# The first MLP product of an encoder block as seven block products

## The reference, cut to what matters

```python
u = _rms(h, norm_mix[l])
proj = u @ w_in[l]                       # latents, convolution input, gates
...
h = h + (g_a * attn + g_c * conv) @ w_out[l]
u = _rms(h, norm_mlp[l])
h = h + jnp.square(jax.nn.relu(u @ w_mlp_in[l])) @ w_mlp_out[l]
return _rms(h, norm_final)[:, N_META:]
```

## Time and profile before

| | |
|---|---|
| median of 3 runs | 1289.13 us (1288.31 to 1291.43) |
| the profiled execution | 1290.69 us |
| its span, first to last instruction | 1289.1 us |
| mean granted TensorE clock | 0.994 |
| PE busy | 1251.3 us, 97% |
| DVE, ACT, POOL busy | 738.5, 490.5, 394.8 us |
| DMA | 146.55 MB, mean 114 GB/s |

### The profile page before, as it was taken

One profiled execution on the slowest core, in us unless ns is written; L12 is line 12 of the kernel. 1 busy time (PEld: TensorE's weight loads), 2 busy tenths in 40 slices (PEclk: granted clock), 3 DMA queues, 4 the chain that ended last, 5 costly groups with the idle time before them and its releaser, 6 DMA issues.

```text
span 1289.1 us, 18449 instructions
## 1 busy us (share of the span) xinstructions
PE 1251.3 (97%) x7037; PEld 1083.4 (84%) x7037; DVE 738.5 (57%) x888; ACT 490.5 (38%) x737; POOL 394.8 (31%) x252
## 2 busy tenths in 40 slices
PE   5999999999999999989999999999999999999997
PEld 4888888888888998878888888888888888887886
DVE  4205999999977877784743123111011136876887
ACT  5234211122256666663522134211222234455455
POOL 1443322233333333326322323344444310020101
PEclk8999999999999999999999999999999999999999
DMA  6222212333220101104344135777777664386443
GB/s 186 69 71 53 76 51 66 90 115 108 87 74 17 35 22 29 49 1 149 109 122 177 66 131 131 181 188 189 187 186 193 137 190 131 131 199 183 125 131 114
DMA packets 145926, 146.55 MB, mean 114 GB/s; under 512 B 11231, under 2 KB 107549, under 8 KB 145868
## 3 DMA queue, kind: packets, MB, share of 16 engines
q1 hardware_dynamic: 132684, 118.48, 29.8%
...
## 4 chain that ended last, share of the span: by engine, by line
PE 86%; issue 4%; DVE 4%; ACT 2%; POOL 2%; DMA 1%; SPq 0%; POOLq 0%; ACTq 0%; DVEq 0%
PE psum L389 55%; PE psum L1918 17%; PE psum L1839 5%; PE psum L1715 3%; PE psum L1745 2%; POOL wlo L376 1%; PE psum L1680 1%; PE psum L1603 1%; PE psum L1727 1%; DMA xt<-in_x_prompt 1%; DVE ptlo L1166 1%; DVE negmax L1154 1%; DVE olo L1231 1%; PE psum L1846 0%; ACT uhi L623 0%
## 5 line engine op out<-in xcount | busy, mean ns | idle before, releaser
L376 POOL TENSOR_TENSOR wlo<-raw,whi 128x1024 fp32r<-128x1024 f32 (+1 forms) x112 | 258.5, 2308 | 511.4 <-ACT whi L371 511.2
L1074 DVE SCALAR_TENSOR_TENSOR psum<-cs,convw,psum 128x799 f32<-128x799 f32 x196 | 189.4, 1048 | 0.0
L371 ACT ACTIVATE whi<-raw 128x1024 fp32r<-128x1024 f32 (+1 forms) x112 | 112.8, 1007 | 123.4 <-PE psum L389 76.0
L1380 DVE SCALAR_TENSOR_TENSOR hid<-psum,rbc 128x768 f32 (+1 forms) x32 | 30.6, 958 | 218.1 <-PE psum L389 218.0
L389 PE MATMUL psum<-uhi,whi 128*128 128x512 f32 x592 | 152.3, 338 | 0.8 <-POOL wlo L376 0.8
L389 PE MATMUL psum<-uhi,wlo 128*128 128x512 f32 x592 | 152.9, 339 | 0.0
L389 PE MATMUL psum<-ulo,whi 128*128 128x512 f32 x592 | 152.6, 339 | 0.0
L389 PE MATMUL psum<-u2hi,whi 128*128 128x512 f32 (+1 forms) x512 | 130.8, 336 | 0.0
L389 PE MATMUL psum<-u2lo,whi 128*128 128x512 f32 (+1 forms) x512 | 130.3, 335 | 0.0
L389 PE MATMUL psum<-u2hi,wlo 128*128 128x512 f32 (+1 forms) x512 | 130.3, 335 | 0.0
L943 ACT ACTIVATE hid<-hid (+1 forms) x32 | 27.1, 847 | 202.3 <-DVE hid L1380 202.3
...
## 6 DMA issues: line engine op xcount, KB each, us to landing
raw<-in_w_in SPq DMA_DIRECT2D x38, 512.0 KB, 4.0
raw<-in_w_mlp_in SPq DMA_DIRECT2D x32, 512.0 KB, 4.1
wsums<-in_w_mlp_out SPq DMA_DIRECT2D x32, 512.0 KB, 7.2
wsums<-in_w_mlp_out POOLq DMA_DIRECT2D x32, 512.0 KB, 7.4
raw<-wsums SPq DMA_DIRECT2D x32, 512.0 KB, 3.3
raw<-in_w_mlp_out SPq DMA_DIRECT2D x24, 512.0 KB, 3.7
...
```

The lines of the kernel that those rows point to most:

```text
L371: nc.scalar.activation(whi[:, c % 2, 0:w], raw[:, c % 4, 0:w], ACT.Copy).then_inc(hi_ready, 1)
L376: gp.tensor_tensor(out=wlo[:, c % 2, 0:w], in0=raw[:, c % 4, 0:w], in1=whi[:, c % 2, 0:w].bitcast(F32), op=ALU.subtract).then_inc(lo_ready, 1)
L1074: ins = nc.vector.scalar_tensor_tensor(out=out, in0=src, scalar=w, in1=a, op0=ALU.mult, op1=ALU.add)
L1380: nc.vector.scalar_tensor_tensor(out=hid[:, ds(i * 4 + c, 1), :], in0=psum[:, pair:pair + 1, 0:TQ], scalar=0.0, in1=rbc[:, :].rearrange("p ...
```

## The change

The first product gets the same form as the second: `IN_MIX` lists seven block products, each eight units of 24 matmuls of 384 columns (256 hidden columns, 512 inputs, 384 tokens). Each product goes to one or two of the four blocks of `hid`: the first visit is a copy by ACT, later ones are additions by DVE, and after the last DVE applies the squared ReLU (`hid_drain`). h is multiplied by 1/rms ahead of its transposition (`h1n`); the spreading matmuls go. The last units of `w_out` are taken by halves of the tokens, so that the norm of the first half can begin. Sums of two blocks of u are made by DVE (`u2_sum`), their parts by ACT and DVE. Weights of both MLP products go through one ring of six slots (`RING`), `unit_used` frees them.

The weight sums of the first product (`isums`) are made in convolution and gates: per unit one copy (SP) and one accumulate (POOL). Those of the second stay in the first 32 units of the first product; the copy of a unit now waits for the copy of the unit ahead of it, since `sum_copy(x // STEPS, x % STEPS)` takes the sums one after the other. Units 32 to 39 of the first product are a `negate` entry.

At the start, five tiles are issued first, the eight vectors go through ACT's queue ahead of its other work, `conv_w` is loaded after unit 3's weights and transposed after the product of unit 2. `MIX` and `SUMS` are in another order. The core of the diff:

```diff
-U_FF = U_IN + KF
 STEPS = 8
+U_FF = U_IN + 7 * STEPS
...
-SUMS = (((0, 0), (1, 0)), ((1, 0), (1, 1)), ((0, 1), (1, 1)), ((0, 0), (0, 1)))
+SUMS = (((0, 1), (1, 1)), ((0, 0), (1, 0)), ((1, 0), (1, 1)), ((0, 0), (0, 1)))
+IN_SUMS = (((1, 0), (1, 1)), ((0, 0), (0, 1)), ((0, 1), (1, 1)), ((1, 0), (0, 0)))
...
+IN_MIX = (
+    dict(a=((1, 0), (1, 1)), b=((0, 0),), to=((1, 0, 1), (1, 1, -1))),
+    dict(a=((1, 1),), b=((1, 0), (0, 0)), sign=-1, to=((1, 0, 1), (0, 0, -1))),
+    dict(a=((0, 0), (0, 1)), b=((1, 1),), to=((0, 0, -1), (0, 1, 1))),
+    dict(a=((0, 0),), b=((0, 1), (1, 1)), sign=-1, to=((0, 1, 1), (1, 1, -1))),
+    dict(a=((1, 1), (0, 0)), negate=True, b=((0, 0), (1, 1)), sign=1, to=((0, 0, 1), (1, 1, -1))),
+    dict(a=((0, 1), (1, 1)), b=((1, 0), (1, 1)), sign=1, to=((0, 0, 1),)),
+    dict(a=((1, 0), (0, 0)), b=((0, 0), (0, 1)), sign=1, to=((1, 1, 1),)),
+)
+IN_UNITS = len(IN_MIX) * STEPS
...
+    dict(a=((0, 0), (0, 1)), b=((1, 1),), to=((0, 0, 1), (0, 1, -1))),
+    dict(a=((0, 0),), b=((0, 1), (1, 1)), to=((0, 1, 1), (1, 1, 1))),
...
+RING = 6
...
-        tapsrows = at("tapsrows", [32, D], F32, V0 + 50176 + 512)
+        tapsrows = at("tapsrows", [32, D], F32, Z0 + 28672)
...
+        mhi = [whx[:], whi[:, 0], whi[:, 1]]
+        mraw = [raw[:, 0], raw[:, 1], raw[:, 2], raw[:, 3], rawx[:, 0], rawx[:, 1]]
+        mlo = [rawlo[:, 0], rawlo[:, 1], rawlo[:, 2], rawlo[:, 3], wlo[:, 0], wlo[:, 1]]
...
+        isums = nc.dram_tensor("isums", [len(IN_SUMS), STEPS, P, KD // 2, 2 * P], F32, kind="Internal").ap()
...
-            for i in X_ORDER[:4]:
+            for i in X_ORDER[:5]:
                 load_x(i)
             columns(win, 0, 0, 0, slice(0, P))
-            sp.wait_ge(vec_clear, 1)
-            for name, (r, n) in VEC.items():
-                sp.dma_start(vecrows[r:r + n, :], t[name][0].rearrange("(k p) -> k p", p=P)).then_inc(consts_landed, 16)
-            sp.dma_start(tapsrows[0:TAPS, :], t["conv_w"][0]).then_inc(taps_landed, 16)
-            for i in X_ORDER[4:]:
+            for i in X_ORDER[5:]:
                 load_x(i)
             for n in range(1, 6):
                 columns(win, 4 * (n // 4), 0, n % 4, slice(n * P, (n + 1) * P))
+                if n == 3:
+                    sp.wait_ge(vec_clear, 1)
+                    sp.dma_start(tapsrows[0:TAPS, :], t["conv_w"][0]).then_inc(taps_landed, 16)
...
+            def in_sum_copy(c, jj):
+                wait_apart(sp, copy_landed[c], jj * 16)
+                sp.dma_start(in_sum_place(c, jj), in_sum_part(c, jj, 0)).then_inc(copy_landed[c], 16)
...
+                wait_apart(sp, copy_landed[c], (jj + STEPS) * 16)
                 sp.dma_start(sum_place(c, jj), sum_part(c, jj, 0)).then_inc(copy_landed[c], 16)
...
+                    in_sum_copy(c, i)
+            rolled(sp, 4, conv_units, peel=1)
             def gate_units(i):
                 for c in range(4):
                     columns(win, U_GATE, i, c, ds(i * (4 * P) + (C_GATE + c * P), P))
+                    in_sum_copy(c, i + 4)
...
-            def in_units(i):
-                for c in range(4):
-                    columns(wi, U_IN, i, c, ds(i * (4 * P) + c * P, P))
-                    sum_copy(c, i)
-            rolled(sp, KF // 4, in_units, peel=1)
-            for m in range(FF_UNITS):
-                if m < 4:
-                    sp.wait_ge(lo_ready, U_FF + m - 3)
+            for x in range(2 * IN_UNITS):
+                if x < 4:
+                    sp.wait_ge(lo_ready, U_OUT + 5 + x)
                 else:
-                    sp.wait_ge(wmlo_ready, m - 3)
-                if m % STEPS == 0 and mix_of(m)[0]["b"] in SUMS:
-                    sp.wait_ge(sums_landed[SUMS.index(mix_of(m)[0]["b"])], 16 * STEPS)
-                sp.dma_start(raw_block(m), wm_block(m, 0)).then_inc(raw_landed[m % 4], 16)
-                if m == 4:
-                    sp.wait_ge(relu_ready, KF)
+                    sp.wait_ge(unit_used, U_IN + x - RING + 1)
+                mix, b = (IN_MIX + MIX)[x // STEPS], x % STEPS
+                if x == 0:
+                    for c in range(4):
+                        sp.wait_ge(sums_landed[c], 16 * STEPS)
+                if b == 0 and x >= IN_UNITS and mix["b"] in SUMS:
+                    sp.wait_ge(sums_landed[SUMS.index(mix["b"])], 2 * 16 * STEPS)
+                sp.dma_start(x_place(x), x_block(x, 0)).then_inc(m_landed[x % RING], 16)
+                if x < 4 * STEPS:
+                    sum_copy(x // STEPS, x % STEPS)
+                if x == IN_UNITS + 8:
...
+            for name, (r, n) in VEC.items():
+                act.dma_start(vecrows[r:r + n, :], t[name][0].rearrange("(k p) -> k p", p=P)).then_inc(consts_landed, 16)
...
-            for j in range(4):
+            for j in range(5):
                 x_rms(j)
             hi_unit(act, 0, 0, 0)
-            x_rms(4)
...
+            def x_negate(x):
+                if x < 2 * IN_UNITS and x_negated(x):
+                    act.wait_ge(m_landed[x % RING], m_count(x))
+                    nc.scalar.activation(mraw[x % RING], mraw[x % RING], ACT.Copy, scale=-1.0).then_inc(wneg_ready, 1)
+            def x_hi(x):
+                if x_negated(x):
+                    act.wait_ge(wsum_landed[x % 3], 16 * summed_before(x + 1, x % 3))
+                else:
+                    act.wait_ge(m_landed[x % RING], m_count(x))
+                act.wait_ge(unit_used, U_IN + x - 2 if x > 0 else U_CO + KD)
+                nc.scalar.activation(mhi[x % 3], mraw[x % RING], ACT.Copy).then_inc(mhi_ready, 1)
...
+            for m in range(IN_UNITS):
+                p, jj = m // STEPS, m % STEPS
+                if m + 2 < IN_UNITS:
+                    x_hi(m + 2)
+                else:
+                    mix_hi(m + 2 - IN_UNITS)
+                for n, (_, _, sign) in enumerate(IN_MIX[p]["to"]):
+                    if in_visits(p, n)[0] == p:
+                        act.wait_ge(unit_used, U_IN + m + 1)
+                        act.wait_ge(h_sq, 2 * NT)
+                        nc.scalar.activation(c_block(m, n), c_banks(m), ACT.Copy, scale=float(sign)).then_inc(hid_copied, 1)
+                x_negate(m + 4)
+                if p + 1 < len(IN_MIX) and jj in (3, 4):
+                    u2_hi(p + 1, jj - 3)
...
+            def hid_drain(m):
+                p = m // STEPS
+                dve.wait_ge(unit_used, U_IN + m + 1)
+                for n, (_, _, sign) in enumerate(IN_MIX[p]["to"]):
+                    visits = in_visits(p, n)
+                    if visits[0] == p:
+                        continue
+                    block_ = c_block(m, n)
+                    dve.wait_ge(hid_copied, max(in_copies(visits[0] * STEPS + m % STEPS + 1), in_copies(m + 1)))
+                    if visits.index(p) > 1:
+                        dve.wait_ge(hid_added, in_adds(visits[visits.index(p) - 1] * STEPS + m % STEPS + 1))
+                    nc.vector.tensor_tensor(out=block_, in0=block_, in1=c_banks(m),
+                                            op=ALU.add if sign > 0 else ALU.subtract).then_inc(hid_added, 1)
+                for n in range(len(IN_MIX[p]["to"])):
+                    if in_visits(p, n)[-1] == p:
+                        block_ = c_block(m, n)
+                        dve.wait_ge(hid_added, in_adds(m + 1))
+                        nc.vector.scalar_tensor_tensor(out=block_, in0=block_, scalar=0.0, in1=block_, op0=ALU.max,
+                                                       op1=ALU.mult).then_inc(hid_whole, 1)
...
+            def in_sum_add(c, jj):
+                gp.wait_ge(copy_landed[c], jj * 16 + 16)
+                gp.dma_start(in_sum_place(c, jj), in_sum_part(c, jj, 1), accum_op=ALU.add).then_inc(sums_landed[c], 16)
...
+            def x_add(x):
+                if x_negated(x):
+                    gp.wait_ge(wneg_ready, negated_before(x + 1))
+                    gp.dma_start(x_place(x), x_block(x, 1), accum_op=ALU.add).then_inc(wsum_landed[x % 3], 16)
+            for x in range(IN_UNITS):
+                gp.wait_ge(mhi_ready, x + 1)
+                gp.tensor_tensor(out=mlo[x % RING], in0=mraw[x % RING], in1=mhi[x % 3].bitcast(F32),
+                                 op=ALU.subtract).then_inc(inlo_ready, 1)
+                if x + 2 < IN_UNITS:
+                    x_add(x + 2)
+                if x < 4 * STEPS:
+                    sum_add(x // STEPS, x % STEPS)
...
-                    pe.wait_ge(taps_landed, 16)
-                    for k in range(KD):
-                        mm = nc.tensor.transpose(bank[:, 7, k * 32:(k + 1) * 32], tapsrows[:, k * P:(k + 1) * P], ident[0:32, 0:32])
-                    mm.then_inc(vec_t, 1)
-            pe.wait_ge(vec_ready, 2)
+            pe.wait_ge(vec_ready, 1)
...
+                if n == 2:
+                    pe.wait_ge(ulo_ready, 2 * KD)
+                    pe.wait_ge(taps_landed, 16)
+                    for k in range(KD):
```

(42 more changed lines are left out.)

364 lines of the change are left out of this document (193 added, 171 removed).

## The result

The changed kernel takes **1319.62 us** in the median (1316.61 to 1322.14, four runs) against 1289.14 of the kernel before: a ratio of 1.0233, 95% interval 1.0207 to 1.0258. It is slower, and above the predicted range (1247 to 1302). The profiled execution took 1319.53 us with a span of 1317.9, 28.8 more than before.

A forecast was written before the change was run, and what follows sets the result against it. The prediction took PE to bound the kernel, with the DMA engines next to watch. Its sum was 1290.7 - 33.3 - 2.5 - 5.5 + 28 = 1277.4, stated as 1277 us, with a range of 1247 to 1302.

The forecast's parts named there:

- The product, -33.3: First MLP product: 192 matmuls fewer on PE at 173.3 ns each, saving 33.3 us.
- Each fits, so I price them at nothing: First product: work of ACT (3.6 us), DVE (3.9) and POOL (3.5) fits in a unit's 4.16 us, cost nothing.
- The second product's handover, -1.2: Start of the second product: its first operand is ready early, which saves PE a wait of 1.2 us.
- The start, -5.5: Kernel start: reordered loads let the first product on PE begin at 16.3 instead of 23.05; -5.5 us, bounds -2 and -7.
- Sums in convolution and gates, 0: Convolution and gates: the added copy and accumulate per unit fit beside the load, costing nothing, bound +5 us.
- The negated product, +8 and the 13 us before it: Units 32 to 39: 13 us from copy 31 to unit 32's start, then +8 us from accumulates issued behind POOL's subtractions.
- T = 5.35 us: First 32 units of the first product: load, copy and accumulate need 5.35 us per unit; bounds 4.6 and 6.25.
- from unit 6 on everything goes at T: First product: once the six-deep ring's lead is spent, units follow the three transfers' period, 5.35 us instead of 4.16.
- 26T - 111: First product: general formula for the whole lag of sums and negated product at transfer period T; +28 us as forecast.
- the forecast case: First product: transfer period T from 4.6 to 6.0 us, kernel at 1258 to 1289 us; chance 0.58.
- Copies one at a time, at their full latency: Rival, first product: each copy lands 7.2 us after issue and sets the unit's period; +76, 1325 us; chance 0.20.
- The transfers are hidden: Rival, first product: three transfers fit into a unit's 4.16 us; 1249 us, or 1257 with the negated product's lag; chance 0.17.

The follow-up runs named there:

- run 6: The kernel of run 4 without the negated sums: sixteen units of the two MLPs multiply by one plain block each; 1255.10 us, ratio 0.9727.
- run 7: The kernel before with only the changed kernel's start (vector rows on ACT's queue, fifth x tile earlier, taps rows later); 1287.14 us, ratio 0.9977.
- run 1: The changed kernel without the 32 weight sums beside the first product; the second MLP multiplies by plain blocks; 1261.03 us, ratio 0.9766.
- run 9: The changed kernel with its 32 accumulates turned into plain copies, copies still waiting one for another; 1307.43 us, ratio 1.0131.
- run 2: The changed kernel with four chains: each copy waits for the copy four units before it, same traffic; 1295.64 us, ratio 1.0033.
- run 10: The changed kernel with its 32 accumulates as plain copies and the one chain of copies broken into four; 1266.15 us, ratio 0.9811.
- run 4: The spread kernel: changed kernel with 16 of the 32 sums beside the output projections, 16 beside every second of the first 32 MLP units; 1262.37 us.

## Why the prediction was wrong

Term by term, in the order of its sum:

- **The product, -33.3 (and -1.3 of the spreading matmuls).** Right in kind. Run 6, which has all of it and neither of the two DMA troubles, shows 270.4 - 242.0 = -28.4. Of the 6 us between, 3.7 are waits for DVE. "Each fits, so I price them at nothing; the cover is thin" was where to look: the three waits stand behind steps on the sums of u that took 3.15 us where 0.96 was taken (run 6), which makes such a unit of DVE's 5.9 us and not 3.9. The squaring of a finished block waits for POOL's subtraction too: 1.3 us in the mean in the changed kernel, 1.6 in the spread one. In the changed kernel none of this shows, since PE's waits there are all for POOL. The squaring's group in the changed kernel from 775 to 1080 us (busy us, mean ns):

```profile
L1515 DVE SCALAR_TENSOR_TENSOR hid<-hid 128x768 f32<-128x768 f32 x31 | 40.5, 1305 | 1.1
```

- **The second product's handover, -1.2.** The rest of the span fell by 0.6.
- **The start, -5.5.** Measured -3.0 (run 7), inside its bounds of -2 to -7. ACT's five squares ended at 12.4, where the prediction had 12.5; the scaled tile was to be there at 13.4 and came at 16.35. DVE's timeline shows what was forgotten (start, us):

```profile
13.98 0.22 DVE L1123 COPY vec<-psum 128x62 f32<-128x62 f32 x1 [1.93 <-PE psum L1760]
...
14.31 2.04 DVE L1114 TENSOR_SCALAR xt<-xt,rstd 128x1024 f32<-128x1024 f32 x1
```

 In DVE's program the copy of the transposed vectors stands ahead of the fifth tile, so that tile waits 1.93 us for PE's transpose of them; and its scaling, of SBUF alone, took 2.04 us where the ones before took 0.75: POOL was at a subtraction from 13.46 to 15.80, and 15.80 + 0.75 is 16.55 for 16.35. The first product began at 18.53 and not at 16.3. A further 2.7 us were won between convolution and first product, which had no term; no run isolates them.
- **Sums in convolution and gates, 0.** Right: 225.8 of 226 us at a share of 0.88.
- **The negated product, +8 and the 13 us before it.** Without crowding it costs 4.0 (run 1 against run 6) to 5.6 us. In the changed kernel its accumulates landed after 6.9 to 8.6 us. The chain of waits from 950 to 999 us has the landings one by one (start, us, what):

```profile
950.44 8.86 DMA raw<-in_w_mlp_in
...
964.45 8.62 DMA raw<-in_w_mlp_in
...
976.99 6.90 DMA rawx<-in_w_mlp_in
```

 The long wait came a unit earlier than predicted. POOL's program has the accumulate of unit 32 ahead of the low half of unit 31, so unit 31 waits for load 32 too, which SP issued behind copy 31 (POOL's accumulate and PE's unit 31, start, us):

```profile
960.68 1.35 POOL L1719 DMA_DIRECT2D raw<-in_w_mlp_in  x1 [11.27 <-ACT raw L998]
...
965.55 0.69 PE L2095 MATMUL psum<-u2hi,whi 128*128 128x384 f32 x1 [11.30 <-POOL rawlo L1723]
```

 The sizes were near. Unit 32 began at 971.8, where the prediction's own way with the measured period gives 775.2 + 5 + 26 x 6.72 + 13 = 967.9, and the waits of PE behind it came to 5.6 us where 8 were taken.
- **T = 5.35 us: this is the step that failed.** The working was throughput: 5.8 us of all engines at a held share of 1.08. As throughput it was right to 2%: when the chain is broken, the period is 5.44 us at a share of 1.09, and an accumulate costs 0.534 x 88/16 = 2.94 us of all engines against the 2.97 predicted (16 were issued in the window of 812 to 900 us; by the 8.70 MB that moved it is 2.83; its queue, in the run of four chains: packets, MB, share):

```profile
q0 software_dynamic: 4519, 8.70, 53.4%
```

 But the program doesn't let the engines be full to that depth. It holds one copy at a time, and the text itself said so ("SP issues copy x only when copy x-1 has landed"), then let "from unit 6 on everything goes at T" with the T of full engines. The period is the larger of the two, and the landing of a copy was the larger: 6.72 us. The row that said it stood in the prediction, the copy's 7.2 us. What set it aside was the argument that in the new order the copy goes ahead of the next load; that was worth half a microsecond at most.
 There is a slip in the sum beside it too. By 26T - 111 the change is worth nothing at T = 5.86, not 6.05, and T = 6.0 gives 1294 and not 1289. It moves the edge of the forecast case, not the forecast.
 Put 6.72 into the formula 26T - 111 and it gives +64 where it gave +28. With -3.0 for the start, and the first product's own 5 us too many (242.0 against 237), the sum is 1290.7 - 33.3 - 2.5 - 3.0 + 64 + 5 = 1320.9; the profiled execution took 1319.5. The 2.7 us won ahead of the first product are in no term, so that the two agree to 1.4 us is in part luck. The 68 us to be found in the first product are 59.6 of the sums' place (run 1), 4.0 of the negated units (run 1 against run 6) and 3.7 of DVE (run 6), 67.3 in all.
- **The rivals.** "Copies one at a time, at their full latency" named the mechanism and its place, and had 0.20. Its period was too high by half a microsecond (7.2 for 6.72), 12 us in 26 steps; that its 1325 is only 5 above the 1320 measured is because the rest of the sum was too low by some 6 us. Its test, "copies at a distance of 7 us and a DMA share under 0.9", held by half: the distance was there, the share was 1.00. Run 9 is the case that this test had in mind. "The transfers are hidden" fell, and for the reason given in kind: T = 4.16 needs 378 GB/s, and with accumulates even four chains carried 292. But the 242 GB/s of the earlier trace rows, read where PE used a unit only every 8.32 us, were no limit, and with plain copies and an unbroken supply 366 GB/s are to be had. A page of the Trainium skill (DMA: Bandwidth & Descriptors, "Anatomy of one DMA") has 436 GB/s for the variable part; the highest rate in the windows shown here is 366, over 88 us.

The share of the loss that is the chain's is a matter of order: taken first it is 25 us of 60 (changed against run 2); with plain copies it is 43 of 50 (run 9 against run 10). Spreading the sums (run 4) removes both.
